# RG-LRU stage of a hybrid mLSTM / RG-LRU / MoE step: second branch's products one place forward, modulation sums at other places, gate rows ahead of the first tile's second direction

## The reference

```python
mod = silu(c) @ w_ada + b_ada                       # 6 x 1024 per stream: shifts, scales, gates
hn = rmsnorm(x, norm1) * (1 + sc1) + sh1
q, k, v, o, gt, xr, gr = split(hn @ w_in)           # gt: 16 gate columns, xr and gr: 512 each
ig, lf = input gate, log_sigmoid(forget gate)       # rows over tokens: 4 heads x 2 directions
h_ml, C, n, m = mlstm_bidir(q, k, v, ig, lf, C0, n0, m0)
xr = dwconv_centred(xr, rg_conv_w, rg_conv_b)       # width 4
for each direction:
    r, i = sigmoid(xr @ wa + ba), sigmoid(xr @ wx + bx)   # block-diagonal, 64 x 64
    a = exp(-8 * r * softplus(-lam))
    h[t] = a[t] * h[t - 1] + sqrt(1 - a * a) * (i * xr)
y_rg = rmsnorm(h_forward + h_backward) * gelu(gr)
x = x + g1 * (concat(y_ml, y_rg) @ w_out)
```

## Time and profile before

| | |
|---|---|
| median of 3 runs | 2016.33 us (2015.13 to 2017.26) |
| the profiled execution: its time | 2010.07 us |
| its span, first to last instruction | 2008.3 us |
| mean granted clock of TensorE | 0.964 |
| TensorE busy, over the span | 1838.7 us (92%) |
| VectorE / ScalarE / GpSimd busy | 1490.5 / 1264.3 / 738.1 us |
| the RG-LRU stage | about 88 to 336 us |

### The profile page before, as it was taken

How to read it: one execution, slowest core, us unless ns; L and a number is a source line. 1 busy time by engine, 2 the same in 40 slices (tenths; PEclk the granted TensorE clock), 3 DMA queues, 4 the chain that set the end, 5 groups by cost and what they waited for, 6 DMA issues and landing times.

```text
span 2008.3 us, 34619 instructions
## 1 busy us (share of the span) xinstructions
PE 1838.7 (92%) x9251; PEld 1418.3 (71%) x9251; DVE 1490.5 (74%) x2060; ACT 1264.3 (63%) x1747; POOL 738.1 (37%) x754
## 2 busy tenths in 40 slices
PE   5887998999999899988999999999999999999950
PEld 2343544799888555667888888888888888888840
DVE  3367554533568668865999999999999999999956
ACT  3353555433224333434888888888888888888842
POOL 3211000000002205452554555654455655555532
PEclk8898999999999999998999999999999999999985
DMA  8733210234402423445885998975777788997977
GB/s 242 263 129 112 78 41 21 84 106 134 109 1 84 153 95 116 168 142 225 302 282 152 331 352 271 338 231 155 217 269 249 268 277 304 321 328 280 314 220 196
DMA packets 121260, 399.55 MB, mean 199 GB/s; under 512 B 28397, under 2 KB 52973, under 8 KB 96237
## 3 DMA queue, kind: packets, MB, share of 16 engines
q1 hardware_dynamic: 75644, 281.66, 37.8%
q0 software_dynamic: 45264, 117.06, 22.1%
q10 hardware_dynamic: 290, 0.02, 0.0%
HBM read 355.47 MB, written 84.60 MB: 219 GB/s over the span
## 4 chain that ended last, share of the span: by engine, by line
PE 48%; DMA 4%; issue 2%; POOL 2%; DVE 2%; ACT 1%; ACTq 0%; DVEq 0%; SPq 0%; POOLq 0%
PE bank L2044 28%; PE bank L2062 14%; PE bank L2031 4%; POOL slot_table L1968 1%; DMA y<-yacc_scratch 1%; PE bank L2051 1%; DMA big<-in_exp_w 1%; DMA yacc_scratch<-y 1%; DVE big L2421 1%; DMA xg<-hn_scratch 0%; DVE big L2413 0%; DVE y L2412 0%; ACTq L1789 0%; DMA yacc_scratch<-y,idx_s 0%; ACT wuph L2177 0%
## 5 line engine op out<-in xcount | busy, mean ns | idle before, releaser
L2306 DVE TENSOR_TENSOR wupl<-big,wuph 128x2048 fp32r<-128x2048 f32 x212 | 485.6, 2291 | 68.9 <-ACT wuph L2177 64.7
L2177 ACT ACTIVATE wuph<-big 128x2048 fp32r (+1 forms) x212 | 404.9, 1910 | 5.3 <-issue 1.3
L2044 PE MATMUL bank<-wuph,xTh 128*128 128x512 f32 x904 | 362.5, 401 | 3.7 <-DVE xTl L2328 3.3
L2044 PE MATMUL bank<-wuph,xTl 128*128 128x512 f32 x904 | 354.8, 392 | 0.0
L2044 PE MATMUL bank<-wupl,xTh 128*128 128x512 f32 x904 | 353.6, 391 | 0.0
L1960 POOL DMA_INDIRECT yacc_scratch<-y,idx_s x105 | 228.3, 2174 | 288.5 <-ACT y L2168 276.4
L1950 POOL DMA_INDIRECT xg<-hn_scratch,idx_g x108 | 243.2, 2252 | 123.4 <-issue 111.9
L2186 ACT ACTIVATE w2h<-w 128x1024 fp32r x210 | 211.1, 1053 | 69.2 <-issue 60.4
L2314 DVE TENSOR_TENSOR w2l<-w,w2h 128x1024 fp32r<-128x1024 f32 x210 | 247.4, 1220 | 8.9 <-ACT w2h L2186 8.4
L2062 PE MATMUL bank<-w2h,hT5h 128*128 128x512 f32 x456 | 189.8, 416 | 17.9 <-ACT y L2168 12.6
L2044 PEld LDWEIGHTS bank<-wuph,xTh 128*128 128x128 f32 x904 | 170.6, 189 | 40.9 <-issue 4.0
(11 more groups left out here) (388 smaller groups left out, 3172.4 us busy)
## 6 DMA issues: line engine op xcount, KB each, us to landing
big<-in_exp_w SPq DMA_DIRECT2D x128, 1024.0 KB, 9.6
w<-in_exp_w SPq DMA_DIRECT2D x64, 1024.0 KB, 11.5
wada<-in_w_ada POOLq DMA_DIRECT2D x16, 1024.0 KB, 6.2
wg<-in_w_in SPq DMA_DIRECT2D x14, 1024.0 KB, 5.3
wada<-in_w_ada SPq DMA_DIRECT2D x4, 2048.0 KB, 14.8
big<-in_w_in SPq DMA_DIRECT2D x8, 1024.0 KB, 5.3
yacc_scratch<-in_consts SPq DMA_DIRECT2D x9, 512.0 KB, 9.8
x<-x_scratch SPq DMA_DIRECT2D x9, 512.0 KB, 4.1
```

The costliest lines, as they stand in the source:

```text
L2044: mm = pe.matmul(b_up[j][:, :], x[:, k, :], w[:, :, k, :], start=(k == 0 and i == 0), stop=(k == KT - 1 and i == 2))
L2177: act.activation(part13(wup[j][0], half), raw13(e % WSLOT, half), ACT.Copy).then_inc(w_high, 1)
L2306: dve.tensor_tensor(part13(wup[j][1], half), raw13(e % WSLOT, half), part13(wup[j][0], half).bitcast(F32), ALU.subtract).then_inc(w_low, 1)
```

## The change

Three things are moved.

1. `gr(0)`, `gr(1)`, `gr(2)` stand behind both directions of tiles 0, 1 and 2, each one place earlier; nothing stands between the directions of tile 3 in their stead. ScalarE's copies move with them. The exponentials of the rows stay in tile 1, now between the copies of `gr(1)`.
2. The modulation sums 1 to 7 are at (0,1): 1 and 2; (1,1): 3 and 4; (2,1): 5; and between the directions of tile 3: 6 and 7. Before they were at (0,0): 1; (0,1): 2 and 3; (1,0): 4; (1,1): 5; (2,0): 6; (2,1): 7.
3. VectorE's L875 to L879 stand in front of direction (0, 1) instead of behind `conv_tile(1)`, with one more count of `row_d`, for which ScalarE waits before it copies `gr(0)`.

The waits follow: `win_used` is raised by two after `xr(3)` (then `gr(1)` is done too), VectorE's waits for `xrp` count the additional copies, and the waits for `row_d` are one higher.

```diff
-        MODS_AT = {(0, 0): (1,), (0, 1): (2, 3), (1, 0): (4,), (1, 1): (5,), (2, 0): (6,), (2, 1): (7,)}
+        MODS_AT = {(0, 1): (1, 2), (1, 1): (3, 4), (2, 1): (5,), (3, 0): (6, 7)}
...
                 if i % 2:
                     pe.wait_ge(full, ring.n)
-                    pe.sem_inc(win_used, 1)
+                    pe.sem_inc(win_used, (i + 1) // 2)
...
                 project(g, (i % 2) * P)
-                if i == 1:
-                    pe.wait_ge(full, ring.n)
-                    pe.sem_inc(win_used, 1)
...
                 if i + 1 < RT:
                     xr(i + 1)
-                else:
-                    gr(i - 1)
...
-                if 1 <= i < RT - 1:
-                    gr(i - 1)
+                if i < RT - 1:
+                    gr(i)
                 if i == N_AT:
 
                     pe.wait_ge(row_a, 6)
-                    pe.wait_ge(row_d, 6)
+                    pe.wait_ge(row_d, 7)
...
                     if d == 0 and i + 1 < RT:
                         xr(i + 1)
-                    elif d == 0:
-                        gr(i - 1)
...
                 if i == 1:
 
+                    act.wait_ge(row_d, 6)
+                if i == 0:
                     act.wait_ge(row_d, 5)
-                if 1 <= i < RT - 1:
-                    gr(i - 1, exp_rows if i == 1 else None)
+                if i < RT - 1:
+                    gr(i, exp_rows if i == 1 else None)
...
-                return 3 if i >= 3 else 0
+                return 3 * max(i - 1, 0)
...
-            rg_dir(0, 1)
-            conv_tile(1)
-
             link(dve.tensor_tensor(m.mn, bb[:, :, :], mx[:, :, :], ALU.subtract))
             dve.wait_ge(zeroed, 2)
             link(dve.tensor_tensor(rows[0:H, :, :], ig, bb[:, :, :], ALU.subtract))
+            dve.sem_inc(row_d, 1)
             link(dve.tensor_copy(ml[:, 0, :], m.mn[:, 0, P - 1:N:P]))
             link(dve.tensor_copy(ml[:, 1, :], m.mn[:, 1, 0:N:P]))
+            rg_dir(0, 1)
+            conv_tile(1)
             rg_dir(1, 0)
```

## The result

| | before | after |
|---|---|---|
| median of 11 runs | 2015.41 us (2013.75 to 2017.26) | 2021.41 us (2019.72 to 2024.79) |
| ratio, with its 95% interval | | 1.0031 (1.0022 to 1.0039) |
| span of the profiled execution | 2008.3 us | 2019.6 us |

The change makes the kernel slower by 6.0 us, where 1.9 us less were forecast; the time lies above the range of 2010.5 to 2018.5.

What follows compares the result with a forecast made beforehand. TensorE, near its limit, was taken to bound the RG-LRU stage; terms of +0.1, +1.1, -4.67, -0.25 and +0.36 gave -3.4 us, and 1.5 us for the clock left -1.9: 2014.4 us, range 2010.5 to 2018.5.

Steps and rivals of the forecast that it cites:

- The term for a pair of sums: Two modulation sums in a row on TensorE take 10.65 us, of which 1.88 is the wait for the bias row.
- the ledger: TensorE's time from the second tile's first branch's end to the last gate products' start: -3.4 us at full clock.
- rival (b): The 1.88 us bias wait vanishes in the second and fourth tiles' pairs: 3.8 us more gained, 2010.6 to 2009.1; 14%.
- the pause at the squares: Fourth tile: TensorE stands still 4.54 us for ScalarE's Square, and the lower clock behind it costs 1.5 us.
- Rival (c): The clock goes down in the fourth tile's pause and stays down through the pair: 5.6 us slower, 2022; 10%.
- to the start of the second tile's branch product: TensorE to the second tile's first gates' end: the hole goes, but what fills it is as long; +0.1 us.
- to the third tile's first gates: Second tile up to the third tile's gates' end: 32.5 us instead of 31.4, the pair having the bias wait; +1.1.
- to the fourth tile's gates' end: Third tile: one modulation instead of two, and second-direction gates without one in front; -4.67 us.
- to the last gates: Fourth tile: pause, squares and pair take 17.29 us instead of 17.54, -0.25, plus 1.5 us for the clock.
- the hole: TensorE's 10.05 us wait for VectorE's convolution ahead of the second tile's gate products, forecast to go.
- the moved rows: VectorE's L875 to L879, 5.52 us, delay direction (0,1) by 0.8 us; 5.0 us of slack makes the move free.
- Rival (d): The stage's end hangs on the final states' landing; a 2 us shift is lost in later waits: 2016.3; 10%.

Runs made afterwards that it cites:

- f1: The changed kernel with the modulation sums at their places of before, only branches and rows moved: 2017.26 us, ratio 1.0012.
- m1: The changed kernel with GpSimd waiting after each bias row's load until it has landed before issuing more: 2018.64 us, ratio 1.0012.
- i1: The changed kernel with sums 2 and 4 behind the second branch's product instead of in front of it: 2010.88 us, ratio 0.9973.
- e1: The kernel before with only the modulation sums at the changed places, branches and rows unmoved: 2021.16 us, ratio 1.0030.
- p1: The changed kernel with the bias rows' loads issued by SP instead of GpSimd: 2014.04 us, ratio 0.9996.
- a1: The changed kernel once more, unaltered, for a second profile: 2023.44 us in one run.

## Why the prediction was wrong

**The term for a pair of sums is the step that failed.** The prediction took 10.65 us for each of three pairs from the one pair of before. They lasted 14.11, 13.42 and 12.07 us, together 7.6 us more, of the 9.6 us by which the ledger was off. The prediction said of the wait in it that "the order of buffers makes each pair's second load wait for the first's buffer in the same way". The mechanism is right, the size is not: the waits are 3.34, 3.12 and 2.49 us instead of 1.88 three times. The pair of before was sums 2 and 3, and that pair waits 1.86 us also in f1; sums 1 and 2 wait 3.25 to 3.35 us in every kernel that has them together with one bias buffer on GpSimd's queue. I had a range for this term that reached below 1.88 (rival (b), the waits vanish) and none that reached above it. The trace of before could have given one: its seven rows took 3.4 to 5.3 us to land, and the one behind the 1.88 us was at the lower end. A landing of 4.8 us in its place would have made the wait 3.3.

**The clock was priced for one pause and came at three.** I set 1.5 us for the pause at the squares and left the waits inside the pairs out, since the 1.88 us pause of before had cost nothing. At 3.1 us and more each of these pauses cost. In the first tile the pair's excess of 3.46 us is 1.46 of wait and 2.0 of products and bias rows at the lower clock, and the branch behind is 16.47 instead of 15.79. In the second tile the excess of 2.77 is 1.24 and 1.5. Rival (c), the slower one, had the right sign and nearly the right time, 2022, but another place: it needed a clock that stays down through the fourth tile's pair, and there it was back during sum 6. That its number came near is luck: it put 8.75 us more (-0.25 + 9.0) between the fourth tile's gates, where 3.3 were measured.

**The ledger, term by term**, forecast and measured against before:

| stretch | forecast | measured | where |
|---|---|---|---|
| to the start of the second tile's branch product | +0.1 | +4.5 | 179.79 - 136.55 = 43.24, against 38.75 |
| to the third tile's first gates | +1.1 | +3.5 | 232.36 - 179.79 = 52.57, against 49.04 |
| to the fourth tile's gates' end | -4.7 | -4.0 | 291.44 - 232.36 = 59.08, against 63.05 |
| to the last gates | -0.25 + 1.5 | +3.3 | 312.25 - 291.44 = 20.81, against 17.54 |
| the last gates | +0.4 | +0.4 | 318.78 - 312.25 = 6.53, against 6.08 |
| sum | -1.9 | +7.8 | |

In the fourth tile 2.9 us are clock (squares 4.14 us for 2.10, and the first half of sum 6 0.9 us longer), twice my 1.5, and 0.6 us a longer wait.

**What was right**: the hole is filled; the moved rows cost nothing (convolution 1 has 9 us of slack in the end, since TensorE came later); the new pause for the Square, 4.59 us for 4.54; the third tile, within 0.7 us; and that the stage's end moves with the last gates (the next stage starts 8.5 us later for 7.8 on the ledger). Rival (d), that the later stages take the difference up, fell: ledger and time move together over all kernels but m1.

**Open.** Why the row of sum 2 takes 4.8 us over GpSimd's queue and that of sum 3 3.4 us, that is, why it lands 1.5 us behind the chunk ahead of it and not 0.2: it isn't the loads behind it, and the order on the queue is the same. The row of sum 2 took 4.7 us in the kernel before too, where it was in no pair, but 3.5 us in i1. Why sums 3 and 4 waited 2.08 us in e1 and 2.86 to 3.12 us elsewhere. The profiled span grew by 11.3 us where the medians differ by 6.0; 2.8 us of it lie behind the stage and were not followed up. The profiled execution of before (2010.07 us) was quicker than each of the 11 runs of the median (from 2013.75), so the two spans overstate the difference.

## What to carry to other kernels

Two pieces that share a buffer want other work between them, not each other: the same sums with 15.8 us of a branch in between wait for nothing. A wait seen once is one sample of a landing time. The other loads of the same kind in the same trace show how far it can go, here 3.4 to 5.3 us. When a change makes three of it, its range has to reach upwards, to the point where the clock falls. And work moved out of a place leaves that place's own wait bare: put something small enough in front of it (here sum 6, 4.3 us, in front of a wait of 4.6).

## What the runs showed of the hardware

- The same load of a 2 KB row landed 3.4 us after its issue by SP (p1) and 4.9 us after its issue by GpSimd behind a 1 MB chunk (the changed kernel), and for this row the GpSimd figure repeated within 0.1 us over the five kernels that have its pair with one buffer. Two rows issued by GpSimd when the chunk ahead was nearly in took 1.7 and 1.8 us.
- Pauses inside a pair of sums of 1.4 to 2.1 us never lowered TensorE's clock in these profiles; of five between 2.49 and 2.55 us three did (a1, i1, m1) and two didn't (the changed kernel, e1); all of 2.86 us and more did. Gates with short pauses can lose the clock too, as f1 shows (no pause over 1.3 us, then 3.49 us for 1.98).
- In m1 the first pair's products, which have only two output rows, took 3.58 us instead of 1.92 behind the pause of 3.25 us, and the bias products that follow them directly took 0.38 us, their time at full clock (0.59 where they ran at the lower one). Nothing else ran on TensorE in between, so the clock came back while only such products ran.
